# One transformer kernel: the end of the expert stage, and the order of long and short matmuls

## The reference

```python
# first block
h = x + concat(forgetting_attention(...), gelu(...) * rg_lru(...)) @ w_out
hn = rms_norm(h, ffn_norm)                        # group top-1, then top-2 of its 8 experts
for e in range(32):
    hid = silu(t @ w_gate[e]) * (t @ w_up[e])     # t: (256, 2048), w_gate[e]: (2048, 256)
    out = out + (hid @ w_down[e]) * comb[:, e:e + 1]
h = h + out
gate = sigmoid(rms_norm(h, ple_norm) @ w_ple_gate)   # (256, 2048) @ (2048, 2048)
h = h + gate * (p @ w_ple_up)
# second block, on h
x = h + concat(diff_attention, moba_attention, dilated_attention) @ w_out   # from rms_norm(h) @ w_in
x = x + memory_cross_attention(rms_norm(x), rms_norm(mem), w_q, w_kv, w_o)
g, u = split(rms_norm(x) @ w_up)                     # w_up: (2048, 11264)
x = x + (silu(conv(g)) * u) @ w_down                 # w_down: (5632, 2048)
return rms_norm(x, g_final)
```

## Time and profile before

| | |
|---|---|
| median of three runs | 2335.27 us (2334.82 to 2345.84) |
| profiled execution, its own time | 2340.84 us |
| its span (first to last instruction) | 2339.0 us |
| granted clock of TensorE, mean | 0.986 |
| PE busy | 2242.4 us, 96% |
| PE's share of the chain that ended last | 88% |
| PE weight loads busy | 1692.4 us, 72% |
| DVE busy | 1315.8 us, 56% |
| ACT busy | 894.8 us, 38% |
| DMA | 519.38 MB, mean 222 GB/s |

### The profile page before, as it was taken

How to read it: one execution, slowest core, us unless ns; L and a number is a source line. 1 busy time by engine, 2 the same in 40 slices (tenths; PEclk the granted TensorE clock), 3 DMA queues, 4 the chain that set the end, 5 groups by cost and what they waited for, 6 DMA issues and landing times.

```text
span 2339.0 us, 30793 instructions
## 1 busy us (share of the span) xinstructions
PE 2242.4 (96%) x11459; PEld 1692.4 (72%) x11459; DVE 1315.8 (56%) x1757; ACT 894.8 (38%) x1197; POOL 25.8 (1%) x32
## 2 busy tenths in 40 slices
PE   9999898899999999899999999979999999999997
PEld 8786777644444443678888878868888888878886
DVE  7795465422222222656666755647777777764443
ACT  4652354311111111535445444435343443433332
POOL 1000000000000000000000000000000000000000
PEclk9999999899999999899999999999999999999999
DMA  8654455499999999456555455535665565555653
GB/s 289 185 164 132 120 180 203 177 383 410 398 410 408 407 408 409 142 190 216 175 168 171 155 161 184 178 107 165 186 188 183 185 188 184 184 188 192 195 192 123
DMA packets 301293, 519.38 MB, mean 222 GB/s; under 512 B 24032, under 2 KB 196096, under 8 KB 292224
## 3 DMA queue, kind: packets, MB, share of 16 engines
q1 hardware_dynamic: 298272, 505.51, 62.5%
q0 software_dynamic: 2912, 12.38, 1.5%
HBM read 515.67 MB, written 5.27 MB: 223 GB/s over the span
## 4 chain that ended last, share of the span: by engine, by line
PE 88%; DVE 7%; ACT 2%; issue 1%; DMA 1%; POOL 0%; DVEq 0%; SPq 0%; ACTq 0%; POOLq 0%
PE acc L649 29%; PE acc L669 23%; PE acc L670 12%; PE ps L1039 9%; PE acc L1061 5%; PE tp L989 3%; PE tp L1001 2%; DVE wlo L1699 2%; PE tp L1002 1%; PE tp L733 1%; PE ps L803 1%; DMA raw<-in_w_in 1%; DVE h L2238 1%; DMA mw<-in_w_expert_up 1%; PE tp L817 1%
## 5 line engine op out<-in xcount | busy, mean ns | idle before, releaser
L669 PE MATMUL acc<-xhl,whi 128*128 128x512 f32 x2496 | 894.2, 402 | 12.9 <-DVE wlo L1699 4.1
L1699 DVE TENSOR_TENSOR wlo<-raw,whi 128x1024 fp32r<-128x1024 f32 x572 | 674.6, 1221 | 221.2 <-ACT whi L1271 217.7
L1271 ACT ACTIVATE whi<-raw 128x1024 fp32r<-128x1024 f32 x572 | 582.3, 1054 | 411.4 <-DMA raw<-in_w_down 141.7
L670 PE MATMUL acc<-xhl,wlo 128*128 128x256 f32 x2496 | 701.9, 281 | 0.0
L669 PEld LDWEIGHTS acc<-xhl,whi 128*128 128x128 f32 x2496 | 471.4, 189 | 130.6 <-issue 6.3
L670 PEld LDWEIGHTS acc<-xhl,wlo 128*128 128x128 f32 x2496 | 473.8, 190 | 0.9 <-issue 0.5
L649 PE MATMUL acc<-whi,xhl 128*128 128x512 f32 x800 | 258.8, 398 | 2.0 <-DVE xhl L1768 1.1
L1039 PE MATMUL ps<-mw,xg 128*64 128x512 f32 x1024 | 229.8, 595 | 2.1 <-DMA mw<-in_w_expert_up 1.3
L2238 DVE TENSOR_TENSOR h<-tp,h 128x512 f32<-128x512 f32 x128 | 87.6, 690 | 172.7 <-PE tp L1002 172.3
L649 PEld LDWEIGHTS acc<-whi,xhl 128*128 128x128 f32 x800 | 152.0, 190 | 42.0 <-issue 6.4
L1039 PEld LDWEIGHTS ps<-mw,xg 128*64 128x64 f32 x1024 | 70.8, 137 | 141.0 <-issue 137.6
(11 more groups left out here) (362 smaller groups left out, 2153.6 us busy)
## 6 DMA issues: line engine op xcount, KB each, us to landing
raw<-in_w_in SPq DMA_DIRECT2D x352, 256.0 KB, 3.0
raw<-in_w_up SPq DMA_DIRECT2D x352, 256.0 KB, 2.9
mw<-in_w_expert_gate SPq DMA_DIRECT2D x128, 512.0 KB, 8.2
mw<-in_w_expert_up SPq DMA_DIRECT2D x128, 512.0 KB, 9.3
mw<-in_w_expert_down SPq DMA_DIRECT2D x64, 1024.0 KB, 12.1
raw<-in_w_down SPq DMA_DIRECT2D x176, 256.0 KB, 3.3
raw<-in_w_out SPq DMA_DIRECT2D x128, 256.0 KB, 3.3
raw<-in_w_ple_gate SPq DMA_DIRECT2D x64, 256.0 KB, 3.6
```

What stands on the lines that cost most here:

```text
L669: pe.matmul(o.rearrange("p (m n) -> p m n", m=2), wh, ahl[:, :, k, :], start=first, stop=False, skip_group_check=True)
L670: return pe.matmul(o[:, S:2 * S], wl, ahl[:, 0, k, :], start=False, stop=last, skip_group_check=True)
L1271: act.activation(whi[:, m % RING, :], raw[:, m % RING, :], ACT.Copy).then_inc(hi_ready, 1)
L1699: dve.tensor_tensor(wlo[:, m % RING, :], raw[:, m % RING, :], whi[:, m % RING, :], ALU.subtract).then_inc(lo_ready, 1)
```

## The change

Two parts.

1. **Order of long and short.** `two_terms` becomes `both_terms`: for one `k` it issues the long matmuls of all tiles first (2 in `features`, 4 in `wide_features`), then the short ones. The matmuls, operands and accumulators are the same.

2. **The end of the expert stage.** The count and the branch stand ahead of the last scatters on PE, and ahead of the adds on DVE. The waits of `after_steps` go into the branch on ACT and DVE. ACT and DVE split chunks 0 and 1 ahead of the last `evict`; chunks 2 and 3 come behind it, on DVE between the parts. The eight last scatters write to six banks (`tp0`, `tp1`, `ps0`, `ps1`, the two halves of `acc1`, then `ps0` and `ps1` again) under two semaphores of their own, `last_done` and `last_added`. Six stand ahead of the first transposes of `h`, two behind them. A part of the transposes waits only for the columns of `h` that it reads. `xT`, a tile used only inside the branch, moves to another place in SBUF.

```diff
-            def two_terms(o, wh, wl, ahl, k, first, last):
+            def both_terms(out, wh, wl, ahl, k, first, last, tiles):
-                pe.matmul(o.rearrange("p (m n) -> p m n", m=2), wh, ahl[:, :, k, :], start=first, stop=False, skip_group_check=True)
-                return pe.matmul(o[:, S:2 * S], wl, ahl[:, 0, k, :], start=False, stop=last, skip_group_check=True)
+                for ct in range(tiles):
+                    pe.matmul(out(ct).rearrange("p (m n) -> p m n", m=2), wh[:, ct * P:ct * P + P], ahl[:, :, k, :], start=first,
+                              stop=False, skip_group_check=True)
+                for ct in range(tiles):
+                    mm = pe.matmul(out(ct)[:, S:2 * S], wl[:, ct * P:ct * P + P], ahl[:, 0, k, :], start=False, stop=last,
+                                   skip_group_check=True)
+                return mm
...
@@ leading @@
                     if c == 0:
                         run_in(idle)
+                        if there_after:
+                            there_after()
...
@@ PE, behind the last pair @@
-            for k in range(8):
-                scatter(PAIRS - 1, k)
-            pe.wait_ge(y_ready, 2 * PAIRS)
-            after_steps(pe)
             pe.wait_ge(ov_list, 1)
             count = pe.value_load(over_i[0:1, 0:1], min_val=0, max_val=MAX_OVER)
             with pe.If(count > 0):
+                pe.wait_ge(y_ready, 2 * PAIRS)
+                after_steps(pe)
...
-            tokens(current, before=leading(h, rows=False))
+            after_steps(pe)
+            def last_scatter(k):
+                pe.wait_ge(y_ready, 2 * (PAIRS - 1) + (1 if k < 4 else 2))
+                if k >= 6:
+                    pe.wait_ge(last_added, k - 3)
+                q = slice(k % 2 * P, k % 2 * P + P)
+                cs = slice(k // 2 * 512, k // 2 * 512 + 512)
+                pe.matmul(last_sum[k], GT[:, (PAIRS - 1) % 2, q], yh[:, cs], start=True, stop=False, skip_group_check=True)
+                pe.matmul(last_sum[k], GT[:, (PAIRS - 1) % 2, q], yl[:, cs], start=False, stop=True,
+                          skip_group_check=True).then_inc(last_done, 1)
+            def last_columns(g):
+                pe.wait_ge(last_added, 2 * (g // 2) + 2)
+            for k in range(6):
+                last_scatter(k)
+            gate_parts = leading(h, last_columns, rows=False, there_after=lambda: (last_scatter(6), last_scatter(7)))
+            tokens(current, before=gate_parts)
...
@@ ACT @@
-            after_steps(act)
-            for k in range(AHEAD):
-                act.wait_ge(w_used, STEPS * PAIRS - STEP + (2 if (n.n + k) % RING >= 4 else 4))
-                split(k)
+            count = act.value_load(over_i[0:1, 0:1], min_val=0, max_val=MAX_OVER)
+            act.wait_ge(w_used, STEPS * PAIRS - STEP + 2)
+            split(0)
+            split(1)
             evict(PAIRS - 1)
...
@@ DVE @@
+            def between_parts(g):
+                if g == 1:
+                    split(2)
+                    last_adds(4)
+                elif g == 2:
+                    split(3)
+                elif g == 3:
+                    last_adds(6)
+                    consume(2)
+                elif g > 3:
+                    by_twos(g)
...
                 if first:
-                    lead(h, hs[:, 1, :], spread=False)
+                    last_adds(0)
+                    last_adds(2)
+                    norm_parts(xh, xl, between_parts)
+                    dve.wait_ge(last_added, 8)
+                    norm_rows(h, hs[:, 1, :], False)
+                    consume(4)
```

More of the change, by code:

```diff
@@ L675, in feature_chunk @@
                 for k in range(4):
-                    for ct in range(2):
-                        w = slice(ct * P, ct * P + P)
-                        mm = two_terms(o[:, ct * 2 * S:(ct + 1) * 2 * S], wh[:, k, w], wl[:, k, w], ahl, 4 * c + k,
-                                       c == 0 and k == 0, c == KT // 4 - 1 and k == 3)
+                    mm = both_terms(lambda ct: o[:, ct * 2 * S:(ct + 1) * 2 * S], wh[:, k, :], wl[:, k, :], ahl, 4 * c + k,
+                                    c == 0 and k == 0, c == KT // 4 - 1 and k == 3, 2)
                 mm.then_inc(chunk_used, 1)
@@ L697, in wide_features @@
                     for k in range(2):
-                        for ct in range(4):
-                            w = slice(ct * P, ct * P + P)
-                            mm = two_terms(o[ct // 2][:, ct % 2 * 2 * S:(ct % 2 + 1) * 2 * S], wh[:, k, w], wl[:, k, w], ahl, 2 * c + k,
-                                           c == 0 and k == 0, c == KT // 2 - 1 and k == 1)
+                        mm = both_terms(lambda ct: o[ct // 2][:, ct % 2 * 2 * S:(ct % 2 + 1) * 2 * S], wh[:, k, :], wl[:, k, :], ahl, 2 * c + k,
+                                        c == 0 and k == 0, c == KT // 2 - 1 and k == 1, 4)
                     mm.then_inc(chunk_used, 1)
@@ L748, in run_in, with leading @@
                     pe.matmul(ps[0][:, 0:P], mean[:, :], mean[:, :], start=True, stop=True, skip_group_check=True)
-            def leading(src, there=lambda g: None, rows=True, idle=0):
+            def leading(src, there=lambda g: None, rows=True, idle=0, there_after=None):
                 k = norms.n
@@ L2283, in _ @@
                 moved(g, 3)
-            evict(PAIRS - 1)
-            for k in range(8):
-                scattered(k)
-            after_steps(dve)
             n.end = N_CHUNKS
-            for k in range(AHEAD):
-                split(k)
             dve.wait_ge(ov_list, 1)
             count = dve.value_load(over_i[0:1, 0:1], min_val=0, max_val=MAX_OVER)
+            split(0)
+            split(1)
+            evict(PAIRS - 1)
             with dve.If(count > 0):
+                after_steps(dve)
                 with dve.Fori(0, count) as i:
@@ L2305, in _, with last_adds @@
                     dve.wait_ge(ov_dve, i * OV_DVE + OV_DVE)
-            h_done()
+            def last_adds(first):
+                for k in range(first, first + 2):
+                    dve.wait_ge(last_done, k + 1)
+                    hh = h[:, k % 2, k // 2 * 512:k // 2 * 512 + 512]
+                    dve.tensor_tensor(hh, last_sum[k], hh, ALU.add).then_inc(last_added, 1)
+            def between_parts(g):
+                if g == 1:
+                    split(2)
+                    last_adds(4)
+                elif g == 2:
+                    split(3)
+                elif g == 3:
[3 more added lines that the diff above has]
+                    by_twos(g)
             gt = Count()
```

13 lines of the change are left out of this document (7 added, 6 removed).

## The result

The changed kernel has a median of 2325.23 us over 12 runs (2322.00 to 2328.85). The kernel before, timed beside it, has 2341.83 us over 12 (2331.98 to 2347.35). The ratio is 0.9941, with a 95% interval of [0.9927, 0.9955]: 13.8 us less (10.5 to 17.1). The two medians lie 16.6 us apart, since the runs of the kernel before scatter (standard deviation 5.0 us, against 2.2); the gain is taken from the ratio here. Forecast were 15.9 less and 2319.4 us, in a range of 2307 to 2330. The time is inside it, 5.8 us above the forecast. Some 3.7 of these are the start: 2325.23 / 0.9941 is 2339.0, not the 2335.27 of three runs. The other 2.1 are the gain.

The account below looks back on a forecast made before the run. PE was taken as the bound, busy 96% of the span, mostly with long and short matmuls. Order 8.2 plus tail 7.7 gave 15.9 us less: 2335.27 to 2319.4 us, range 2307 to 2330.

Parts of the forecast that it names:

- A: The forecast itself, both edits gaining as computed: own range 2313 to 2327 us, chance 0.53.
- the sum of a group: Two longs then two shorts on PE: 226.7, 118.5 and 353.5 ns sum to 698.7, against 707 before.
- the surplus as belonging to each change of length: Matmul time on PE beyond long and short alone arises where lengths alternate; 8.3 ns a pair in the usual pace.
- Rival C: The whole surplus of the long and short matmuls goes: 2309.6 us, chance 0.12.
- its count: Over 2560 pairs, one in seven already in the better pace, the new order saves 8.2 us.
- Rival B: The order of long and short is of no account, paces may hang on phase: 2327.6 us, chance 0.19.
- the branch: Count and branch on PE behind the last down matmul end at 941.44, so scatters start 1.5 us late.
- Rival D: The tail's branch waits for instructions behind weight transfers, scatters start 4.5 us later still: 2323.9 us, chance 0.11.
- the clock: In the tail, four scatters run at 1.2 GHz and two at 2.4; gate chunks 0 to 3 at 2.4.
- the waits for DVE: PE waits for DVE's parts 5, 6 and 7 among the first gate chunks: 0.4, 1.3 and 0.4, together 2.15 us.
- The tail's sum: End of the expert stage: gate chunk 3 ends at 963.9 instead of 971.6, 7.7 us less.
- Rival E: Back-to-back short matmuls expose their weight loads, short to short 190 ns instead of 118.5: 2403 us, chance 0.05.

Follow-up runs that it names:

- the blocks of eight: The changed kernel with eight long, then eight short matmuls per chunk of `features` instead of two and two: 2327.68 us, ratio 0.9957.
- The part alone: The kernel before with only `both_terms` in place of `two_terms`, its expert tail as before: 2334.45 us, ratio 0.9990.
- the tail alone: The changed kernel with `two_terms` back, so only the end of the expert stage changed: 2333.56 us, ratio 0.9980.
- Other orders: The changed kernel with eight long then eight short matmuls (2327.68 us), or with long, short, short, long for two tiles (2326.09 us).

## Why the prediction was right, and where it was not

**Sign, size and range** held: 13.8 less measured, 15.9 forecast, and the time in A's own range of 2313 to 2327. Some of that is luck: edit 1 was put too high and edit 2 too low, and within both, terms that were wrong cancelled.

**Edit 1, the sum of a group.** 698.7 ns forecast, 697 measured, but two of its parts were wrong and cancelled. Long to long was put at the 226.7 of the earlier trace rows, and is 233; short to short at 118.5, and is 115; a long-short and a short-long together at 353.5, and are 349 (233 and 116). So "the surplus as belonging to each change of length" failed: in groups of two longs cost 233 with a long or a short one behind them, and the blocks of eight have three quarters fewer changes of length and the same pace. There the longs come down to 226.4 to 226.8 from the sixth on, so the surplus is tied to short ones nearby, but not by a fixed amount for each change. What makes it stays open; the accumulator half and the two pieces of the operand are of no account. Rival C, the whole surplus gone at 690 a group, is out.

**Edit 1, its count.** This is the step that was furthest off, 8.2 us forecast where 4.7 is what the traces give. "One pair in seven is in the better pace" was an estimate from one profiled execution, and the pace isn't a property of the place: the loop with over half of the pairs took it in two executions of four. Averaged over all sets of four pairs that took under 360 ns a pair, which leaves out waits and the low clock, the four executions of the kernel before have 352.2, 348.2, 352.2 and 348.8 ns a pair, mean 350.3; the changed kernel has 348.5. That is 1.8 ns x 2560 = 4.7 us, not 8.2; against an execution in the worse pace 9.4 us, against one in the better nothing. With four executions the share of the two paces, and so the 4.7, is an estimate. The part alone measured 3.0 us by the medians and 2.3 by the ratio. Rival B named the ground ("they may hang on phase"). The rule that the prediction cited beside it (Trainium skill, "TensorE: Matmul & The Clock Gate", "Back-to-back issue gap": the columns over the clock and 2.5 ns) has one pace for both orders; the trace disagrees, with 346.7, 348.3 and 353.3 ns for the same columns. The prediction left out that the section calls this the gap of an isolated matmul, and says that in a stream the weight loads set the spacing too.

**Edit 2, the branch.** Put 1.5 us late "near the late end", it was hidden: first scatter 2.66 us behind the last down matmul, as before. The forecast let it begin when the last down matmul starts, 0.60 us ahead of its end; the load of the count began 4.4 us ahead of that end, 3.8 us sooner. Rival D's time is out, but its mechanism has something for it: in the seven executions with the branch among the down matmuls it took 4.67 to 5.55 us, with 370 GB/s of DMA beside it in two of them, and in the five with the old tail 3.35 to 3.69, with 5 GB/s in the first; among the scatters, at 33 GB/s, 3.49. That the transfers are the cause is not shown. The margin is small: in the tail alone, where the branch took 5.55 us, it ended 0.2 us ahead of the first scatter, in the others 0.9 to 1.5.

**Edit 2, the clock.** Four scatters at 1.2 GHz were forecast, all six ran so in the first profile; that took back what the branch gave (first gate chunk 10.8 forecast 10.9). Over the executions it is 0, four or six of them, and 8.0, 9.5 or 10.8 us. Before, the tail had 13.7 to 17.1 us at 1.2 GHz, the gate's first chunk in it: without the idle 4.6 us that second fall is gone. By the chains it had cost some 3.0 us, an estimate: the first gate chunk takes 5.36 before and 3.02 after, the transposes ahead of it 1.10 where they take 0.45 at 2.4 GHz.

**Edit 2, the waits for DVE.** 2.15 forecast, 1.3 measured, at the place named. With the splits moved 0.2 is left.

**The tail's sum.** 7.7 forecast, 7.7 in the first pair of profiles (34.1 to 26.4), 8.8 between means (34.2 over the four of the kernel before, 25.5 over the tail alone and the changed kernel twice; the two of "Other orders" have the same tail, at 25.0 and 24.8). With the 4.7 of edit 1 that is 13.5, against 13.8 and 13.6 measured. Of the parts alone the order fits: 4.7, against 2.3 (-0.5 to 5.1). The tail does not on its face: 8.8, against 4.7 (0.9 to 8.2). It would come near, at 5.7, if ten of its twelve runs were in the worse pace and half of those of the kernel before: at the same mean clock (0.985 and 0.986) as others at 2334.4 to 2334.8, two stand 9 us lower, as far as the paces are apart. That is argued from times; only one of the twelve was profiled, in the worse pace.

**Rival E**, the weight loads exposed, is out: 115 ns from short to short.

## What to carry to other kernels

Profile a kernel more than once before a pace is read as a property of its code: a stream of matmuls of unequal length can settle at one of two paces, and an edit that looked worth 1.4% of a loop was worth about half, because half of the profiled executions had it already. A branch belongs where its engine's sequencer has work queued ahead of it and the engine then waits for another one anyway; short matmuls put ahead of it "for nothing" brought 3.92 us of it into the open. An idle stretch of PE can cost twice, itself and the lower clock behind it, so that removing it from a chain can be worth more than its length.

## What the runs showed that was not expected

- Long and short in turns, equal code and clock: 346.7 or 353.3 ns a pair, held through a stretch of up to 1340 pairs (some 470 us), another one in another execution. What sets it was not found. The distances repeat every three pairs, in the execution shown first 118, 241, 120, 236, 113 and 232 ns.
- The branch on PE took 3.35 to 3.69 us in the old tail and 4.67 to 5.55 among the last down matmuls, where nobody waited for it.
- 32 filler matmuls of 128 columns ahead of a branch made the kernel 7 us slower: 3.92 us of issue, where the same branch without them showed none, and 1.06 behind six scatters.
- Behind the same 2.7 us without a matmul the granted clock stayed at 2.4 GHz in one execution and was at 1.2 for 3.4 or 6.8 us in others. Over the 12 runs of the changed kernel the time falls by 1.6 us for each 0.001 of mean granted clock (2320.2 us of span at 0.988, 2327.0 at 0.984).
